# Two MoE layers in one kernel: tokens gathered once per layer in expert order, the combine one pair behind, one spare chunk buffer less

## What is computed

```python
def expert_block(args):
    xb, e = args
    hu = xb @ w_in[e]                       # 1024 -> 512 gate + 512 up
    return (jax.nn.silu(hu[:, :EXPERT_FF]) * hu[:, EXPERT_FF:]) @ w_out[e]

y = y_buf[dest] * flat_w[order][:, None].astype(y_buf.dtype)
out = jnp.zeros_like(ht).at[token_of].add(y)
```

## Time and profile before

| | us |
|---|---|
| median of 3 runs | 1376.23 (1376.09 to 1378.11) |
| span of the profiled execution | 1378.2 |
| first MoE layer, first gate matmul to the end of the last combine | 241.0 to 729.8 |
| second MoE layer, the same | 883.2 to 1372.1 |

### The profile page before, as it was taken

The page is one execution under the profiler, slowest core; times in us unless marked ns, Lnnn a source line. Parts: engine busy times, 40 slices in busy tenths (PEclk is TensorE's granted clock), DMA queues, the critical chain, the costliest instruction groups (busy, mean ns, idle before and its releaser), DMA issues.

```text
span 1378.2 us, 14140 instructions
## 1 busy us (share of the span) xinstructions
PE 1279.1 (93%) x5854; PEld 614.6 (45%) x5854; DVE 387.7 (28%) x572; ACT 184.6 (13%) x487; POOL 18.8 (1%) x23
## 2 busy tenths in 40 slices
PE   6949998999999999999999999899999999999997
PEld 5836655333444343333434455544334333444342
DVE  4318544223222222222222141422222223222222
ACT  1000011111111111111112131111111111111110
POOL 0000010000000000000000100000000000000000
PEclk9979998999999999999999999899999999999999
DMA  9865353799999999999999626398999999999995
GB/s 324 239 124 216 123 183 123 293 343 384 394 393 393 394 395 395 395 395 393 393 386 387 218 113 221 127 396 298 395 395 395 395 393 394 394 394 393 393 393 201
DMA packets 203718, 447.09 MB, mean 324 GB/s; under 512 B 16656, under 2 KB 19128, under 8 KB 203664
## 3 DMA queue, kind: packets, MB, share of 16 engines
q1 hardware_dynamic: 202688, 443.70, 86.5%
q0 software_dynamic: 976, 2.63, 1.3%
HBM read 443.68 MB, written 2.62 MB: 324 GB/s over the span
## 4 chain that ended last, share of the span: by engine, by line
PE 84%; DVE 4%; ACT 3%; issue 1%; DVEq 0%; ACTq 0%
PE ps L1000 83%; ACT work L488 2%; PE ps L1003 2%; DVE work L903 1%; DVE work L725 0%; DVE work L715 0%; DVE xs L937 0%; DVE work L643 0%; DVE work L710 0%; DVE work L708 0%; ACT work L478 0%; DVE work L896 0%; DVE work L726 0%; DVE xs L651 0%; DVE work L892 0%
## 5 line engine op out<-in xcount | busy, mean ns | idle before, releaser
L1000 PE MATMUL ps<-ring,work 128*64 128x512 f32 (+1 forms) x3456 | 855.2, 594 | 2.3 <-ACT work L478 1.5
L1000 PEld LDWEIGHTS ps<-ring,work 128*64 128x64 f32 (+1 forms) x3456 | 294.2, 144 | 521.6 <-issue 514.5
L1000 PE MATMUL ps<-work 128*128 128x128 f32 (+4 forms) x1730 | 320.9, 348 | 63.1 <-ACT work L488 24.1
L1000 PEld LDWEIGHTS ps<-work 128*128 128x128 f32 (+2 forms) x1730 | 224.2, 195 | 166.5 <-issue 109.4
L488 ACT ACTIVATE work<-ps,wcol 128x128 f32<-128x128 f32 x256 | 73.2, 368 | 327.3 <-PE ps L1000 327.3
L885 DVE RECIPROCAL work<-work 128x512 f32<-128x512 f32 x32 | 107.3, 3353 | 1.1
L883 DVE TENSOR_SCALAR work<-work 128x512 f32<-128x512 f32 x32 | 13.7, 428 | 332.1 <-ACT work L535 332.1
L903 DVE COPY work<-ps 128x256 f32<-128x256 f32 x32 | 13.6, 425 | 287.3 <-PE ps L1003 287.3
L535 ACT ACTIVATE work<-ps 128x512 f32<-128x512 f32 x32 | 19.1, 597 | 343.9 <-PE ps L1000 343.9
L543 ACT COPY work<-ps 128x512 f32<-128x512 f32 x64 | 37.5, 586 | 189.8 <-PE ps L1000 189.8
L1000 PE MATMUL ps<-work,ring 128*128 128x256 f32 x256 | 57.6, 388 | 1.3 <-DVE work L638 1.3
(11 more groups left out here) (110 smaller groups left out, 247.0 us busy)
## 6 DMA issues: line engine op xcount, KB each, us to landing
ring<-in_moe_w_in SPq DMA_DIRECT2D x120, 2048.0 KB, 17.5
ring<-in_moe_w_out SPq DMA_DIRECT2D x60, 2048.0 KB, 18.9
ring<-in_hg_w_in SPq DMA_DIRECT2D x7, 2048.0 KB, 20.6
work<-in_moe_w_in SPq DMA_DIRECT2D x4, 2048.0 KB, 9.0
ring<-in_moe_w_in SPq DMA_DIRECT2D x8, 1024.0 KB, 14.7
ring<-in_moe_w_out SPq DMA_DIRECT2D x8, 1024.0 KB, 14.4
ring<-in_w_kv SPq DMA_DIRECT2D x4, 2048.0 KB, 19.7
ring<-in_hg_w_out SPq DMA_DIRECT2D x2, 2048.0 KB, 11.7
```

What stands on the lines that cost most here:

```text
L1000: return pe.matmul(o, l, r, start=start, stop=stop)
```

## The change

- `places` (DVE, once per layer) works out where each token stands when the tokens are sorted by expert: the first slot of each expert by a prefix sum over the counts (two matmuls for the counts with experts on partitions, one for the sum), and a matrix `place` (256 tokens x 512 slots) of zeros and ones. It also writes `win`, the first slot of each expert as an integer, moved back for the last experts so that 64 columns fit.
- `sorted_gather` (TensorE, once per layer) multiplies `hn` with `place`: 16 matmuls of 128x128 by 128x512, in two groups of 8 (16 records each), both in pair 0. ScalarE (`sorted_columns`) writes the eight results, scaled, to `xc`.
- For pairs 1 to 15 TensorE no longer gathers. ScalarE (`windows`) reads each expert's first slot into a register and copies 64 columns of `xc` (8x64 elements per partition) to `xgT`, two copies per pair. Pair 0 is gathered as before.
- The combine of pair u now stands in pair u+1, between the up matmuls and `hidden_T`; that of the last pair stands behind the loop.
- `spread_T` stands behind `hidden_T`, ahead of `down`, and has bank 4 to itself.
- `xc` takes one of the two spare buffers. So only load 8 goes to a spare buffer, and loads 9 to 17 take ring slots.

```diff
 def in_extra(r, it):
-    return is_int(it, 0) and r in (RING, RING + 1)
+    return is_int(it, 0) and r == RING
...
-                elif is_int(it, 0) and r < 2 * RING + 2:
-                    sp.wait_ge(*expert_read(layer, r - RING - 2, it))
+                elif is_int(it, 0) and r < 2 * RING + 1:
+                    sp.wait_ge(*expert_read(layer, r - RING - 1, it))
                 else:
                     sp.wait_ge(*expert_read(layer, r - RING, it))
...
+                    for x2 in range(2):
+                        e = it * (2 * UN) + (2 * u + x2)
+                        at = act.value_load(win[0:1, layer, bass.ds(e, 1)], min_val=0, max_val=2 * T - BLK)
+                        act.copy(xgT[:, u % 2, :, x2 * BLK:(x2 + 1) * BLK],
+                                 xc[:, :, bass.ds(at, BLK)]).then_inc(xg_ready, 1)
...
+                        if first:
+                            for k in range(KD // 2, KD):
+                                sorted_columns(k)
+                            windows(it, 1)
...
+                mm(ps[0:E, 0, 0:P], asg[:, 0, :], ones[:], True, False)
+                mm(ps[0:E, 0, 0:P], asg[:, 1, :], ones[:], False, True).then_inc(countT_done, 1)
...
+                pe.wait_ge(countT_ready, layer + 1)
+                mm(ps[:, 1, 0:E], countT, before[0:E, 0:E]).then_inc(first_done, 1)
...
+                        for a in range(TT):
+                            i = mm(ps[:, k % 4, :], hn[:, a, k * P:(k + 1) * P], place[:, a, :], a == 0, a == TT - 1)
+                        i.then_inc(cg_done, 1)
...
-                        if not last:
-                            gather_next(it, u + 1, 0)
+                        if first:
+                            sorted_gather(range(KD // 2))
+                        else:
+                            combine(it, u - 1, is_int(it, 0) and u == 1, False)
                         pe.wait_ge(hid_ready, it * UN + (q + 1))
+                        hidden_T(5, ht_done)
+                        pe.wait_ge(pickw_ready, it * UN + (q + 1))
                         if not n0:
                             pe.wait_ge(s_ready, it * UN + q)
-                        hidden_T(5, ht_done)
-                        if not last:
-                            gather_next(it, u + 1, 1)
+                        spread_T(4, st_done)
                         pe.wait_ge(hidT_ready, it * UN + (q + 1))
...
+                        if first:
+                            sorted_gather(range(KD // 2, KD))
```

More of the change, by code:

```diff
@@ L207, in ring_chunk @@
         def ring_chunk(layer, r, it):
-            return MOE[layer] + r - (0 if is_int(it, 0) and r < RING else 2)
+            return MOE[layer] + r - (0 if is_int(it, 0) and r < RING else 1)
         def gate_or_up(layer, r, it):
-            c = extra[r - RING] if in_extra(r, it) else chunk(ring_chunk(layer, r, it))
+            c = extra if in_extra(r, it) else chunk(ring_chunk(layer, r, it))
             return c.rearrange("p (k n) -> p k n", n=512)
@@ L531, in body @@
                         last = last_pair(it, u)
+                        first = is_int(it, 0) and u == 0
                         act.wait_ge(up_done, it * (2 * UN) + (2 * q + 1))
@@ L535, in body @@
                         act.activation(en, ps[:, 6, :], ACT.Exp, scale=-1.0).then_inc(exp_done, 1)
-                        if not last:
-                            gathered(it, u + 1, 0)
-                            gathered(it, u + 1, 1)
+                        if first:
+                            for k in range(KD // 2):
+                                sorted_columns(k)
+                        elif not last:
+                            windows(it, u + 1)
                         for half in range(2):
@@ L834, in over @@
                 with dve.If(n > 1):
+                    for a in range(TT):
+                        dve.tensor_scalar(pos[:, :, a, :], tpos[:, a, :].rearrange("p (q e) -> p q e", e=2), -1.0,
+                                          None, ALU.add).then_inc(s["base"], 1)
+                    dve.wait_ge(s["base"], TT)
                     dve.memset(mark[:, 2:3], 0.0).then_inc(s["x"], 1)
@@ L921, in moe @@
                 passes(layer)
+                places(layer)
                 def body(it):
@@ L1262, in body @@
                             down(c, 1, down_done)
-                            pe.wait_ge(pickw_ready, it * UN + (q + 1))
-                            spread_T(5, st_done)
-                        pe.wait_ge(s_ready, it * UN + (q + 1))
-                        for a in range(TT):
-                            for half in range(2):
-                                if a == 0:
-                                    pe.wait_ge(y_ready, it * (2 * UN) + (2 * q + 1 + half))
-                                i = mm(ps[:, 2 * a + half, :], spread[:, a * P:(a + 1) * P],
-                                       y[:, half * 512:(half + 1) * 512], is_int(it, 0) and u == 0, last)
-                            i.then_inc(c_done, 1)
+                        if first:
+                            sorted_gather(range(KD // 2, KD))
                 over_pairs(pe, body)
+                combine(ITERS - 1, UN - 1, False, True)
                 over(layer)
```

134 lines of the change are left out of this document (98 added, 36 removed).

## The result

The changed kernel takes 1391.5 us (median of 4 runs, 1389.8 to 1393.7) against 1377.2 for the kernel before on the same chip (1376.1 to 1379.0): a ratio of 1.0103, 95% interval 1.0089 to 1.0118. It is slower by 14 us; 1387 was forecast, in a range of 1380 to 1396.

A forecast was written before the change was run, and what follows sets the result against it. PE (30.75 us a pair) and transfers (31.9) were taken as bounds 1% apart. Load 18 8.4 us later and a longer last chain gave +5.5 us per layer: 1378.2 + 11 - 2.0, about 1387, range 1380 to 1396.

The forecast's parts named there:

- Two bounds 1% apart, the transfers just behind: MoE pairs before the change: PE 30.75 us, weight transfers 31.9 at 394 GB/s; PE 3.9 us late at layer end.
- A later pair becomes 25.9 us of work and 31.9 of time: Pairs after pair 0: PE work falls 4.8 us from 30.75, but PE then waits for loads.
- Load 18 8.4 us later: Pair 0 at 39.5 us plus pair 1 at 25.9 free load 18's slot at 65.4 us, against 57.0.
- rival (a): PE's clock falls while it waits between pair 0 and pair 1: 2.8 us per fall, 1393 to 1398; chance 0.18.
- The small matmuls cost 0.5 us: Three matmuls for counts and prefix sum ahead of each layer's first gate matmul: 0.5 us, between 0 and 1.0.
- The spare buffer costs nothing: Loads ahead of load 18 fill idle transfer time, so giving up one buffer is free; otherwise 5.4 us per layer.
- Last landing 8.1 us later, chain of 19.2 us behind the up columns: Layer end: last load lands at 1369.1, but PE's work after the up weights land runs to 1377.6 and decides.
- +5.5 us per layer: Layer end at 1377.6 against 1372.1; the first layer taken to be the same, so +11.0 in all.
- From the profile to the median: Whole kernel: profiled span 1378.2 + 11 = 1389.2, less 2.0 because the median of runs stood lower: 1387.2.
- Rival (b): Weight transfers exceed 394 GB/s when PE reads less: 1.3% faster gives 1376, 2% about 1370; chance 0.11.
- (c): PE alone bounds the MoE layers, transfers keeping up with 25.9 us pairs: 58 us less per layer, 1260; chance 0.01.
- (d): ScalarE's windows or DVE's `places` deliver columns later than bounded: 4 us more per layer, 1395 and up; chance 0.10.

The follow-up runs named there:

- 5: Kernel before, with the second layer's gathers for pairs 3 to 15 cut to a quarter: 1374.0 us, ratio 0.997.
- 3: Changed kernel, with the second layer's combines in the loop (pairs 3 to 10) cut from 512 to 64 columns: 1389.2 us.
- 4: Changed kernel, with the second layer's sorted gather computing 64 of 512 slots: 1381.2 us.
- 1: Kernel before, with one spare chunk buffer instead of two and nothing else: 1377.4 us, ratio 1.000.
- 2: Changed kernel, with three extra 128x512 matmuls, result unread, filling PE's wait between pair 0 and pair 1: 1386.2 us.
- 12: Changed kernel, with the combine between the gate and up matmuls from pair 4 on: 1390.0 us.
- 11: Changed kernel run once more, unedited, in a later session: 1388.1 us, ratio 1.008 against the kernel before.
- 6: Kernel before, with only the combine moved one pair behind (gathers per pair, two spare buffers, no sorted gather): 1374.8 us, ratio 0.998.
- 10: Kernel before, combine one pair behind, from pair 4 on between gate and up matmuls, earlier behind the up matmuls: 1370.0 us, ratio 0.994.

## Why the prediction was right, and where it was off

- **Two bounds 1% apart, the transfers just behind.** Right, and shown from both sides: 35 us less for PE gained 3.5 in the kernel before (5), 21 us less gained nothing in the changed one (3).
- **A later pair becomes 25.9 us of work and 31.9 of time.** Right: pair 1 took 27.5, of which 1.6 is a clock fall, so 25.9 of work, and the late pair 31.9.
- **Load 18 8.4 us later.** It was 9.6 (66.7 against 57.0). Pair 0 by itself took 39.1 where the sum said 39.5: the two windows cost less than put down, 2.7 us of waiting in all, since the second window's register load hides behind the first one's copy (1.26 us for both, with 0.66 of idling ahead, where 2.5 was put down). What was added is the clock fall in pair 1, 1.6 us, which the prediction had as rival (a) and not in the sum. That the end of the layer follows pair 0 one for one was shown by 4 (9.0 for 9.0).
- **The small matmuls cost 0.5 us.** They cost less. From the matmuls for the positions to the gate matmuls it is 9.1 us before (874.08 to 883.19) and 9.3 after (877.42 to 886.75) in the second layer, 9.6 and 9.5 in the first.
- **The spare buffer costs nothing.** Right (1), for the reason given.
- **Last landing 8.1 us later, chain of 19.2 us behind the up columns.** The 8.1 hold the 0.5 ahead of the gate, so 7.6 by the count used here; measured 7.9. That is luck in part: load 18 was 1.2 us later than forecast, but from its issue to the last landing the stream took 1.8 us less than before, where the sum had 0.8. The 1.0 between is not explained. The up columns' last part landed at 475.0 and the end was at 494.3, 19.3 behind. PE reached the matmuls that want it 0.3 us after the landing, held up by its own chain behind the wait of pair 14 (51.1 us, 2.7 of it a clock fall); the two chains end together here.
- **+5.5 us per layer.** From the first gate matmul on that is 5.0. Measured 5.4 in the second layer (5.8 in the second profile), and the first was short: 496.0 against 488.8, +7.2 (+6.9 in the second profile). Load 18 is late there by 9.9 us, and its first gap also has to take the attention bias, which the bounds had at 0 to 2.6 us. The mis-sized term is the first layer, taken to be the same as the second. Of the 1.8 us between them 1.6 lie in the stream: the up columns' last part lands at 476.6 in the first layer, at 475.0 in the second. The bias load is issued at 293.5, 11 us ahead of load 18, and in the 7 us behind load 18 the transfers' share is 1.01, where the second layer has 0.82: the gap was full. That fits the bias load; no run takes it away, so its part is argued and not shown.
- **From the profile to the median.** Wrong as an argument, without harm to the number. The span of the profiled execution of before stood 2 us over the median, and I moved the forecast down by as much. Later executions show the time to be 1.8 us over the span each time, so this execution was a slow one, some 3.8 over the median. The place is seen in the rows: its clock was low for 20.4 us in the first mixer, and its first MoE layer began at 241.0, where in the other profiles it begins between 237.1 and 239.1. But 1378.2 + 11 - 2.0 is nothing else than the median of before, 1376.2, with the 11 us of the two layers, and that is the right sum. What does mislead are the two profiles side by side: 1388.0 - 1378.2 = 9.8 understates the 12.6 us (5.4 + 7.2) that the layers themselves lost.
- **Rival (b), a faster stream.** Excluded: 394 GB/s with PE busy 27 us of 31.9, as with 29.4 of 30.7.
- **Rival (a).** Half right: the fall comes, and costs 1.6 and not 2.8 at its first place. In the pairs of the middle it costs nothing that could be measured: they take 31.9 us with it, and in 3 PE's clock in the second layer is lower still (0.94 in place of 0.95) at the same length of the layer. In a layer's last chain it can cost, as the rival said: some 1.3 us in the first layer of 2 (its end is 20.6 behind the landing of the up columns, in place of 19.3) and 1.6 in that of 12.
- **Rivals (c) and (d).** (c) is excluded by the late pair of 31.9 us. (d) is too: the sorted gather starts at 900.63, right behind the up matmuls, so `places` was in time, and the windows took less than put down.

Open: why the changed kernel's executions spread over 6 us (1387.1 to 1393.7) where those of before spread over 3. The clock falls come or stay away at the same place (first layers of 3 and 11), but each run has only one profile, so their share in the spread was not measured.

## What to carry to other kernels

Where the engine and the transfers lie within a few per cent of each other, work taken from the engine is worth only the slack between them at the end; read that slack from the last landing and the matmul that uses it before counting instructions. What then decides is the last moment at which the stream stands still for want of a free slot, which has to be looked for again after each edit, and at the other end the longest chain of the engine's work behind any wait for a load, not only behind the last one. A gather made once for all is paid at the worst place, in the pair that frees the first slots; the part of the change that was worth keeping (6, and 10 as its best form) is the one that moved work without adding any to that pair.

## What the runs showed of the hardware

- In the changed kernel the clock fell to 0.50 again and again (so granted from 277.3 to 280.6 us, in pair 1 of the first layer) while PE waited 2.0 to 4.2 us for weights or windows, though it was at full work on both sides; 32 records of 128x512 then took 8.5 to 10.0 us in place of 7.1. It did not fall in each such wait: behind one of 3.6 us in the first layer of 2 the 32 records took 7.09. Before the change there were no such waits, and the granted clock was 1.00 over both MoE layers. The Trainium skill, "TensorE: Matmul & The Clock Gate", section "HAM oscillation — how this bites in real kernels", tells of such falls in waits for data. The trace agrees, with the waits and durations just given.
- What the falls would cost was mostly taken from time in which PE would have waited anyway: the late pairs kept their 31.9 us.
- The rate of the stream did not depend on what PE did: 387 GB/s for gate and up chunks and 404 to 413 for down chunks in both kernels, 394 over a pair.
- ScalarE's copy of 8 runs of 64 columns from a place in a register took 0.63 us for 512 elements per partition, 0.04 more than a plain copy of 512 from PSUM (0.59). Of two in a row, the second one's register load was hidden behind the first copy.
